# Two attentions of a fused fp32 block: waits, the place of a reciprocal, and the product with the values in two halves

## What is computed

```python
def one_block(qi):                      # first layer; blocks of 128 queries
    s = jnp.einsum('bqkgd,bskd->bkgqs', qi, k, preferred_element_type=jnp.float32) * scale
    p = jax.nn.softmax(s, axis=-1)
    return jnp.einsum('bkgqs,bskd->bqkgd', p.astype(v.dtype), v)
...
for blk in range(seqlen // ATT_BLOCK):  # second layer, causal
    s = jnp.einsum('bhqd,bhkd->bhqk', q[:, :, q0:q1], k[:, :, :q1]).astype(jnp.float32) * scale
    s = s + fcum[:, :, q0:q1, None] - fcum[:, :, None, :q1]
    s = jnp.where(kpos[None, :] <= qpos[:, None], s, -jnp.inf)
    prob = jax.nn.softmax(s, axis=-1)
    outs.append(jnp.einsum('bhqk,bhkd->bhqd', prob.astype(v.dtype), v[:, :, :q1]))
```

## Time and profile before

| | |
|---|---|
| time, median of 3 runs | 2623.56 us |
| lowest and highest | 2619.59 and 2625.0 us |
| span of the profiled execution | 2619.9 us |
| PE busy | 2539.2 us, 97% |
| DVE, ACT, POOL busy | 1587.0, 1233.5, 1132.0 us |
| first attention, first to last row maximum | 256.9 to 457.6 us |
| second attention | about 1855 to 2345 us |

### The profile page before, as it was taken

How to read it: one execution, slowest core, us unless ns; L and a number is a source line. 1 busy time by engine, 2 the same in 40 slices (tenths; PEclk the granted TensorE clock), 3 DMA queues, 4 the chain that set the end, 5 groups by cost and what they waited for, 6 DMA issues and landing times.

```text
span 2619.9 us, 33861 instructions
## 1 busy us (share of the span) xinstructions
PE 2539.2 (97%) x12946; PEld 2112.9 (81%) x12946; DVE 1587.0 (61%) x2413; ACT 1233.5 (47%) x1858; POOL 1132.0 (43%) x754
## 2 busy tenths in 40 slices
PE   5999999999999999999999999999999999999998
PEld 3788788777888888878788888888888888888886
DVE  7654889578555566575833366666666666655333
ACT  4343888445444443333533345543656656652132
POOL 0222434437878774444487334233322222235233
PEclk8999999999999999999999999999999999999999
DMA  6134000432222126553233322222111111157342
GB/s 271 65 121 129 1 1 1 142 101 83 94 77 92 73 100 226 192 177 109 107 113 121 121 73 89 81 69 93 57 53 53 49 49 57 60 206 279 146 185 97
DMA packets 84465, 275.89 MB, mean 105 GB/s; under 512 B 9392, under 2 KB 9520, under 8 KB 84304
## 3 DMA queue, kind: packets, MB, share of 16 engines
q1 hardware_dynamic: 84304, 273.71, 29.8%
HBM read 219.54 MB, written 54.13 MB: 104 GB/s over the span
## 4 chain that ended last, share of the span: by engine, by line
PE 81%; DVE 10%; ACT 5%; issue 2%; POOL 1%; DMA 0%; DVEq 0%; SPq 0%; ACTq 0%; POOLq 0%
PE ps L609 12%; PE ps L611 11%; PE ps L610 11%; PE ps L977 7%; PE ps L978 7%; PE ps L979 7%; PE ps L848 5%; PE ps L829 4%; PE ps L1034 3%; PE ps L1036 3%; PE ps L1035 3%; DVE wf L3047 2%; PE ps L805 2%; PE ps L806 2%; DVE st L2573 1%
## 5 line engine op out<-in xcount | busy, mean ns | idle before, releaser
L3374 POOL TENSOR_TENSOR hl<-raw,hl 128x1024 fp32r<-128x1024 f32 x161 | 403.6, 2509 | 929.9 <-ACT hl L1393 929.9
L609 PE MATMUL ps<-ht,hl 128*128 128x512 f32 x1552 | 633.7, 408 | 10.5 <-DVE ht L2444 5.4
L611 PE MATMUL ps<-ht,hl 128*128 128x512 f32 x1552 | 608.4, 392 | 0.0
L610 PE MATMUL ps<-ht,hl 128*128 128x512 f32 x1552 | 608.2, 392 | 0.0
L609 PEld LDWEIGHTS ps<-ht,hl 128*128 128x128 f32 x1552 | 293.6, 189 | 71.3 <-issue 6.2
L611 PEld LDWEIGHTS ps<-ht,hl 128*128 128x128 f32 x1552 | 293.0, 189 | 63.7
L610 PEld LDWEIGHTS ps<-ht,hl 128*128 128x128 f32 x1552 | 294.0, 189 | 54.2 <-issue 1.7
L3451 POOL TENSOR_SCALAR wf<-wf,st 128x1024 f32<-128x1024 f32 (+2 forms) x192 | 167.9, 874 | 343.1 <-DVE st L2581 287.4
L1393 ACT ACTIVATE hl<-raw 128x1024 fp32r<-128x1024 f32 x163 | 171.4, 1053 | 182.2 <-PE ps L1036 66.5
L2384 DVE TENSOR_TENSOR ps<-ps,wf 128x512 f32<-128x512 f32 x116 | 80.8, 697 | 152.1 <-PE ps L979 151.9
L829 PEld LDWEIGHTS ps<-cst,wf 128*128 128x128 f32 x1088 | 126.6, 141 | 56.2 <-issue 34.4
(11 more groups left out here) (287 smaller groups left out, 5298.5 us busy)
## 6 DMA issues: line engine op xcount, KB each, us to landing
raw<-in_wst SPq DMA_DIRECT2D x243, 512.0 KB, 4.0
wf<-scratch_rows SPq DMA_DIRECT2D x32, 512.0 KB, 5.0
scratch_g<-wf SPq DMA_DIRECT2D x22, 512.0 KB, 2.6
wf<-scratch_g SPq DMA_DIRECT2D x44, 256.0 KB, 4.4
wf<-in_xT SPq DMA_DIRECT2D x16, 512.0 KB, 8.0
htf<-in_wst SPq DMA_DIRECT2D x16, 512.0 KB, 15.4
scratch_ys<-wr SPq DMA_DIRECT2D x16, 512.0 KB, 4.8
ht<-scratch_ys SPq DMA_DIRECT2D x32, 256.0 KB, 6.0
```

What stands on the lines that cost most here:

```text
L609: self.op.matmul(out, wh, xh[:, c], start=(j == 0), stop=False)
L610: self.op.matmul(out, wh, xl[:, c], start=False, stop=False)
L611: t = self.op.matmul(out, wl, xh[:, c], start=False, stop=(j == kt - 1))
L3374: self.op.tensor_tensor(K.hl[:, u * 2048 + 1024:u * 2048 + 2048], K.raw[:, i % 3 * 1024:(i % 3 + 1) * 1024], hi.bitcast(F32), ALU.subtract ...
```

## The change

Four things are changed:

- Waits that other waits imply are dropped, on all engines, in both attentions: on ACT `scores`, `weighed(g-16)` and one half of `turn(g-4)` ahead of the exponential; on DVE `exp(g-16)`, `weighed(g-16)` and `turn(g)`; on PE `phi` where `plo` is waited for, and `top` where `exp` is; on POOL `exp` where `rd` is.
- In the first attention, PE waits for `weighed(s)` ahead of the last of the four matmuls of `scores(s+2)`, and not after them, ahead of `turn(s)`.
- In the first attention, DVE makes the reciprocal of unit s+1 in step s right behind the maximum of unit s+2; before, the reciprocal of unit s+2 came at the end of step s.
- In the first attention, the sixteen matmuls of a product are split: the key blocks 0 to 3 in the even step, 4 to 7 in the odd step after it. The copy on ACT and the addition on DVE move to the end of the odd step. The last product, in step 64, stays whole.

```diff
--- before.py
+++ after.py
@@ -790,7 +790,7 @@
         self.last_tails()
         self.mark("stage", "project1")
 
-    def scores(self, A, g, h, qt, q, kh, kl, causal, ready):
+    def scores(self, A, g, h, qt, q, kh, kl, causal, ready, weighed=None):
         K = self.K
         nk = (qt + 1) * 128 if causal else 1024
         pair = g % 2
@@ -803,6 +803,8 @@
             for label in ready:
                 self.wait_ge(*K.at(*label))
             self.op.matmul(out, qs, K.wrr(kh)[:, c], start=True, stop=False)
+            if c.stop == nk and weighed is not None:
+                self.wait_ge(*K.at("weighed", A, weighed))
             t = self.op.matmul(out, qs, K.wrr(kl)[:, c], start=False, stop=not diag)
             if diag:
                 self.consts()
@@ -810,7 +812,7 @@
                 t = self.op.matmul(K.ps[pair][:, nk - 128:nk], K.idr[:, :], K.maskr[:, :],
                                    start=False, stop=True)
         t.then_inc(*self.done("scores", A, g))
-        free = (("top", A, g),) if causal else (("top", A, g), ("exp", A, g))
+        free = (("top", A, g),) if causal else (("exp", A, g),)
         for half in range((nk + 511) // 512):
             self.emptied[2 * pair + half] = free
 
@@ -829,25 +831,28 @@
                 t = self.op.transpose(K.ps[2][:, o:o + 128], K.w(p)[:, j * 128:(j + 1) * 128],
                                       K.c_id)
             t.then_inc(*self.done("turn", A, g, half))
-            self.emptied[4 + bk] = (("phi", A, g, half), ("plo", A, g, half))
-
-    def back(self, A, g, qt, hi, lo, v, causal, ready):
+            self.emptied[4 + bk] = (("plo", A, g, half),)
+
+    def back(self, A, g, qt, hi, lo, v, causal, ready, js=None):
 
         K = self.K
         nk = qt + 1 if causal else 8
         for gg in (g - 1, g):
             for half in range((((qt if gg == g else qt - 1) + 1 if causal else 8) + 3) // 4):
-                self.wait_ge(*K.at("phi", A, gg, half))
                 self.wait_ge(*K.at("plo", A, gg, half))
         for label in ready:
             self.wait_ge(*K.at(*label))
-        self.bank_free(6)
-        for j in range(nk):
+        js = js or range(nk)
+        if js[0] == 0:
+            self.bank_free(6)
+        for j in js:
             c0 = 128 if causal and j == qt else 0
             for n, m in enumerate((hi, lo)):
                 t = self.op.matmul(K.ps[3][:, c0:256], K.wrr(v)[:, j * 128:(j + 1) * 128],
                                    m[:, j, c0:256], start=(j == 0 and n == 0),
                                    stop=(j == nk - 1 and n == 1))
+        if js[-1] < nk - 1:
+            return
         t.then_inc(*self.done("product", A, g // 2))
         self.emptied[6] = (("out", A, g // 2),)
 
@@ -858,7 +863,7 @@
             h, qt = s // 8, s % 8
             k = 8 if h < 4 else 10
             self.scores(1, s, h, qt, h, k, k + 1, False, (("stacklo", "q", h // 2), ("stacklo", "q", 4),
-                         ("stackhi2", "q", 4, 1)))
+                         ("stackhi2", "q", 4, 1)), s - 2 if s >= 2 else None)
 
         for s in range(-2, 66):
             if s + 2 < 64:
@@ -867,10 +872,11 @@
                 self.spread(23, 0, "tok", ())
             if 0 <= s < 64:
                 self.turn(1, s, s % 8, 18 + s % 4, False)
-            if s >= 2 and s % 2 == 0:
-                hi, lo, _ = pt1(K, ((s - 1) // 2) % 2)
-                self.back(1, s - 1, (s - 1) % 8, hi, lo, 12 + (s - 1) // 32, False,
-                          (("vstack", 1),))
+            if 2 <= s < 65:
+                g = s // 2 * 2 - 1
+                hi, lo, _ = pt1(K, (g // 2) % 2)
+                js = range(8) if s == 64 else range(4 * (s % 2), 4 * (s % 2) + 4)
+                self.back(1, g, g % 8, hi, lo, 12 + g // 32, False, (("vstack", 1),), js)
             if s == 22:
                 self.sums([22], [("toksq", 3)], 1, 3, "tok", 1)
             yield
@@ -1630,18 +1636,14 @@
         nk = (qt + 1) * 128 if causal else 1024
         m, den = (K.st[:, 4 * (g % 16) + j:4 * (g % 16) + j + 1] for j in range(2))
         pw = K.w(p)[:, 0:nk]
-        self.wait_ge(*K.at("top", A, g))
         if causal:
             self.wait_ge(*K.at("minus", A, g))
         else:
-            self.wait_ge(*K.at("scores", A, g))
+            self.wait_ge(*K.at("top", A, g))
             if g >= 4:
-                for half in (0, 1):
-                    self.wait_ge(*K.at("turn", A, g - 4, half))
+                self.wait_ge(*K.at("turn", A, g - 4, 1))
             else:
                 self.wait_ge(*K.at("tok", 2 if g < 2 else 3))
-        if g >= 16:
-            self.wait_ge(*K.at("weighed", A, g - 16))
         self.op.activation(pw, pw if causal else K.ps[g % 2][:, 0:nk], ACT.Exp, bias=m, scale=1.0,
                            accum_out=den).then_inc(*self.done("exp", A, g))
 
@@ -1679,9 +1681,9 @@
                 self.att_square(slice(0, 768), 0, 30)
                 for n in (0, 1):
                     self.tok_high(n, 0)
-            if s >= 2 and s % 2 == 0:
-                h = (s - 1) // 8
-                self.back(1, s - 1, h, (s - 1) % 8, K.htlf(4 + h // 2))
+            if 3 <= s < 64 and s % 2 or s == 64:
+                g = s // 2 * 2 - 1
+                self.back(1, g, g // 8, g % 8, K.htlf(4 + g // 16))
             if s in (4, 8, 12, 16):
                 j = s // 4 - 1
                 self.wait_ge(*K.at("tok", 3))
@@ -2558,8 +2560,6 @@
         m = K.st[:, 4 * (g % 16):4 * (g % 16) + 1]
         ps = K.ps[g % 2][:, 0:nk]
         self.wait_ge(*K.at("scores", A, g))
-        if g >= 16:
-            self.wait_ge(*K.at("exp", A, g - 16))
         if causal:
             pw = K.w(p)[:, 0:nk]
             if g >= 3:
@@ -2591,7 +2589,6 @@
             src = v3(K.ps[2][:, bk * 512:bk * 512 + len(js) * 128])
             q = slice((qt % 2) * 128, (qt % 2) * 128 + 128)
             r = slice(js[0], js[-1] + 1)
-            self.wait_ge(*K.at("turn", A, g, half))
             self.wait_ge(*K.at("phi", A, g, half))
             self.op.tensor_tensor(lo[:, r, q], src, hif[:, r, q],
                                   ALU.subtract).then_inc(*self.done("plo", A, g, half))
@@ -2609,6 +2606,8 @@
         for s in range(-2, 66):
             if s + 2 < 64:
                 self.top(1, s + 2, (s + 2) // 8, (s + 2) % 8, 0, False)
+            if 0 <= s + 1 < 64:
+                self.soft(1, s + 1)
             if s == 40:
                 self.wait_ge(*K.at("toksq", 3))
                 self.copy_out(8, 1, 23, "tok")
@@ -2618,11 +2617,9 @@
                 self.att_square(slice(0, 768), 0)
             if 0 <= s < 64:
                 self.turn(1, s, s % 8, pt1(K, (s // 2) % 2), False)
-            if s + 2 < 64:
-                self.soft(1, s + 2)
-            if s >= 2 and s % 2 == 0:
-                h = (s - 1) // 8
-                self.back(1, s - 1, h, (s - 1) % 8, K.htlf(4 + h // 2))
+            if 3 <= s < 64 and s % 2 or s == 64:
+                g = s // 2 * 2 - 1
+                self.back(1, g, g // 8, g % 8, K.htlf(4 + g // 16))
             if s == 22:
                 self.reciprocal(8, "tok")
             yield
@@ -3446,7 +3443,6 @@
         nk = (qt + 1) * 128 if causal else 1024
         rd = K.st[:, 4 * (g % 16) + 2:4 * (g % 16) + 3]
         pw = K.w(p)[:, 0:nk]
-        self.wait_ge(*K.at("exp", A, g))
         self.wait_ge(*K.at("rd", A, g))
         self.op.tensor_scalar(pw, pw, rd, 0.0, ALU.mult,
                               ALU.add).then_inc(*self.done("weighed", A, g))
```

## The result

The changed kernel takes 2635.43 us (median of 4 runs, 2633.57 to 2636.32), the kernel before 2624.28 us beside it. The ratio is 1.0047, with a 95% interval of 1.0032 to 1.0061. In profiled executions the span went from 2619.9 to 2633.7 us.

A forecast was written before the change was run, and what follows sets the result against it. PE was taken as the bound, with three engines near their limit in the first attention. Terms 10.3 + 1.0 + 0.5 - 0.5 - 1.5 = 9.8 us gave 2633.4 against the median; own range 2627 to 2641, 8 in 10: 2620 to 2641.

The forecast's parts named there:

- the ring of one step: First attention: scores, maximum, reciprocal, weighing, last score matmul, next maximum form a new ring of 3.08 us a step.
- the addition in the odd step: First attention: next maximum queues behind an addition waiting for ACT, 3.37 us and not 3.08; pairs 0.37 to 0.39 longer.
- the last score matmul that waits for the weighing: Sign in the first attention's profile: each unit's last score matmul on PE waits for POOL, about 0.2 and 0.5 us.
- the odd heads' reciprocal: DVE, first attention: after an odd head's addition the reciprocal is held, 1.26 us after the maximum, not 1.12, once a pair.
- The sum: Whole kernel: 10.3 + 1.0 + 0.5 - 0.5 - 1.5 = 9.8 us slower, 2633.4 against the median.
- the 27 pairs of the prediction: First attention: of 32 pairs of steps 27 counted as regular, each 0.38 us longer, 10.3 us together.
- The 3.7 between span and median of the kernel before: Kernel before: shown median 2623.56 lies 3.7 us above the profiled execution's 2619.9, put down to runs scattering by 5 us.
- Part 1: First attention: product halves take the low part off PE's way at the turn; 0.50 us a pair goes.
- Rival A: First attention: weighing is in time, PE's work and the addition bound the pair at about 5.85 us; 2614 us; 10%.
- Rival B: First attention: ring holds but addition is not in its way, pairs 6.16 or 6.30; no change, 2625.5 us; 20%.
- Rival C: First attention: PE's longer standing brings the clock to its lower level, costing 50 us and more; 4%.
- The five sums of squares on POOL: First attention: 2.38 us each between weighings, making the next weighing 0.14 late four times and 0.43 in step 43; together 1.0.

The follow-up runs named there:

- heads exchanged: Changed kernel with the outputs of even and odd heads of the first attention exchanged, so even heads are written from partition 64 on: 2636.65 us, measured once.
- the kernels with the old reciprocal: Changed kernel with the reciprocal back at the end of the step: 2614.21 us without PE's early wait for weighed, 2612.75 with it; with addition behind next maximum, two banks: 2607.85.
- the late addition: Changed kernel without PE's early wait for weighed, addition moved behind the next maximum and reciprocal, products alternating between banks 6 and 7: 2609.28 us, ratio 0.9948.
- the four without the early wait: Changed kernel minus PE's wait for weighed before the last score matmul: alone 1.0017; old reciprocal 0.9963; addition behind next maximum, two banks 0.9948; both 0.9941.

## Why the prediction was right, step by step

The mechanism was right, and the traces show it: the ring of one step, the addition in the odd step, and the last score matmul that waits for the weighing, foretold at 0.2 and 0.5 late and measured at 0.25 and 0.50 on even heads. That the forecast of the time, 2633.4, came within 2 us of the median is in part luck, since a term was missed and three estimates were off, and by the spans the miss is 4.0 us; the items below say where.

- **The ring of one step** was foretold at 3.08 and measured at 3.11. Maximum to reciprocal is 1.14 (289.72 to 290.86) and not 1.12; in the odd-head rows below POOL starts 0.09 after the reciprocal (373.03 to 373.12), the maximum 0.03 to 0.04 after the scores. Experiments: without the wait the pair drops by 0.29; with the reciprocal back it drops to 5.77 with or without the wait.
- **The addition in the odd step** was foretold at 3.37 on both heads; it is 3.36 on even heads. On odd heads it is 3.51: 0.14 was missed, the one wrong term of that chain. It sits on ACT, at the copy. ACT of the kernel after, on an even head, and then ACT and DVE on an odd one:

```profile
291.13 1.12 ACT L1647 ACTIVATE wf<-ps,st 128x1024 f32<-128x1024 f32 x1
292.13 0.21 ACT L1647 ACTIVATION_READ_ACCUMULATOR wf<-ps,st 128x1 f32 x1
292.22 0.37 ACT L1670 ACTIVATE htf<-ps 64x256 f32<-64x256 f32 x1
```

```profile
372.88 0.15 DVE L2579 RECIPROCAL st<-st 128x1 f32<-128x1 f32 x1
...
373.12 1.13 POOL L3447 TENSOR_SCALAR wf<-wf,st 128x1024 f32<-128x1024 f32 x1 [1.99 <-DVE st L2579]
373.14 1.12 ACT L1647 ACTIVATE wf<-ps,st 128x1024 f32<-128x1024 f32 x1
...
374.14 0.21 ACT L1647 ACTIVATION_READ_ACCUMULATOR wf<-ps,st 128x1 f32 x1
374.31 0.19 PEld L808 LDWEIGHTS ps<-wr 128*128 128x128 f32 x1 [0.52 <-POOL wf L3447]
...
374.38 0.38 ACT L1670 ACTIVATE htf<-ps 64x256 f32<-64x256 f32 x1
...
374.79 0.43 DVE L2601 TENSOR_TENSOR htf<-ps,htf 64x256 f32<-64x256 f32 x1 [0.57 <-ACT htf L1670]
375.24 1.22 DVE L2573 TENSOR_REDUCE st<-ps 128x1 f32<-128x1024 f32 x1
```

On the even head the copy starts 0.09 after the accumulator's read began, while that still runs; on the odd head 0.24 after, when it has ended. The rows from which 1.10 was read (exponential to copy) were an even head's. The 0.45 from addition to maximum held (374.79 to 375.24), and the page's rule on start quadrants ("VectorE: DVE Perf Modes" of the Trainium skill, "Two Vector instructions with no wait between them") gave the 0.12 to 0.14 of the odd heads' reciprocal: 3.23 against 3.11, and the trace agrees. The prediction calls that reciprocal the first instruction on DVE to touch SBUF from partition 0 again; it is the first to read there, for the maximum ahead of it has already written `st` from partition 0. With the heads exchanged the longer step to the reciprocal went along: 1.26 from the maximum (287.75 to 289.01) on an even head, 1.14 (363.22 to 364.36) on an odd one.
- **The sum.** The first attention grew by 13.9 us (210.7 to 224.6) where 11.3 was foretold (10.3 + 1.0 + 0.5 - 0.5). Counted from the maxima of the two traces, the 27 pairs of the prediction, sums of squares included, grew by 11.7 us where 11.3 was foretold: the 0.14 missed on odd heads is in ten of them, some 1.5 us, and is mostly made up for by an early pair that got 0.3 shorter (7.19 to 6.88) and by the squares, which cost less than foretold. The rest lies in what was only estimated: the first two pairs grew by 1.7 (0.5 was taken), the two around step 22 by 0.5 (nothing was taken), and from the last pair on it was 0.1 (0.5 less was taken). The second attention gave 1.8 (492.1 to 490.3) where 1.5 was taken. In the profiled executions the stages between took 1.9 more (1385.7 and 1387.5), which nothing of the change touches; over all traces of this study that stretch lies between 1385.7 and 1389.5, so it is scatter. By medians the whole is 11.2 against 9.8 foretold, by the ratio 12.3, by the two spans 13.8. The 3.7 between span and median of the kernel before, put down to scatter, is not all scatter: in every run whose span is on record the device time is about 1.8 above it.
- **Part 1** was right: the low part is off PE's way, and alone with the dropped waits the halves make the kernel 0.37% faster.
- **Rival A** (the weighing in time) did not happen in the changed kernel; it is what the kernels with the old reciprocal do. They also show that its price, 5.85 a pair, was near (5.77 and 5.91). **Rival B** named the addition as not in the way: the late addition shows that it is. **Rival C** fell with the clock at 1.00. The five sums of squares on POOL were priced at 1.0; in the trace the weighings behind three of them began 0.08, 0.36 and 0.11 late, together 0.55. Those behind the other two, on odd heads with their longer steps, began on time.

## What to carry to other kernels

When a step is moved later on one engine, list what used its result and when: here the reciprocal had a step to spare, and the move gave that away together with the weighing behind it, and made of maximum, reciprocal, weighing and one score matmul a ring that runs once per step. Measure such a ring by adding start to start along it before counting what each engine has to do: PE was busy 91% and DVE 81% of the steady part, and the pace was that of the ring. And a copy or addition that waits for another engine belongs behind the next instruction that has all it needs, with a second bank to hold its input; that was worth more (6.18 and 6.46 to 5.71 a pair, against 0.07) than all waits dropped.

## What the runs showed of the hardware that was not expected

ScalarE too starts an instruction later when it writes from another partition on. In the changed kernel the copy to partitions 64 to 127 began 0.02 to 0.03 after the end of the accumulator's read before it, and the copy to partitions 0 to 63 began 0.10 to 0.12 before that end: 14 pairs of odd heads and 16 of even heads, without exception. With the heads exchanged all 16 copies of even heads began 0.02 to 0.03 after the read and all 14 of odd heads 0.12 before its end. In the five other kernels that have both the halves and a copy right behind the read (the four without the early wait, and the old reciprocal with it), all 14 copies of odd heads began 0.02 to 0.03 after the read, all 16 of even heads 0.10 to 0.15 before its end. The copy reads PSUM from partition 0 on either head, so it is the place of the output that makes the difference; against which earlier access ScalarE holds it is open.

The dropped waits together were worth 0.07 a pair in the first attention and 1.8 us over 490 in the second (one trace of the kernel before, 492.1, against nine with the waits dropped, 490.2 to 490.4). Which of them gave it was not measured apart.
